# Residual rows kept transposed through the tail: scatter added to feature rows, norm factors applied behind the projections, gated outputs handed over one step later

## What is computed

```python
xl_new = xl + gt1 * (mix_l @ w_out)
xl_new = xl_new + gt2 * expert_choice_ffn(...)          # scatter: zeros.at[idx].add(ye)
x = rmsnorm(xl_new, g_final)                            # end of the first block
# even layer
h = rms_norm(x, g_in); z = h @ w_in                     # z: cq, ckv, kpe, q_s, k_s, v_s, gate
q = rms_norm(cq, g_q_a) @ w_q_up; kv = rms_norm(ckv, g_kv_a) @ w_kv_up
x = x + (concat(o_mla, o_swa) * silu(gate)) @ w_out
# odd layer
h = rms_norm(x, g_in); z = h @ w_in                     # z: q, k, v, forget logits, gate
x = x + (o * silu(gate)) @ w_out
out = rms_norm(x, g_final_2)
```

## Time and profile before

| what | value |
|---|---|
| time, three runs | 1425.26, 1425.86, 1425.97 us |
| profiled execution, its own time | 1426.7 us |
| span of its trace | 1424.9 us |
| PE, DVE, ACT, POOL busy | 991.3, 341.5, 245.9, 94.7 us |
| transfers | 483.21 MB, mean 339 GB/s |

### The profile page before, as it was taken

The page is one execution under the profiler, slowest core; times in us unless marked ns, Lnnn a source line. Parts: engine busy times, 40 slices in busy tenths (PEclk is TensorE's granted clock), DMA queues, the critical chain, the costliest instruction groups (busy, mean ns, idle before and its releaser), DMA issues.

```text
span 1424.9 us, 14616 instructions
## 1 busy us (share of the span) xinstructions
PE 991.3 (70%) x6385; PEld 490.5 (34%) x6385; DVE 341.5 (24%) x810; ACT 245.9 (17%) x501; POOL 94.7 (7%) x87
## 2 busy tenths in 40 slices
PE   5998876666565656665665576555655688889977
PEld 3855822212121111111111111111111587779875
DVE  4766500000001000000000000000000647645574
ACT  3534100000000000000000000000000546434442
POOL 1300000000020000000000000000000363100020
PEclk9999988878887787878878778888887799989999
DMA  9995689999999999999999999999998341144411
...
DMA packets 34992, 483.21 MB, mean 339 GB/s; under 512 B 3886, under 2 KB 3888, under 8 KB 5744
## 3 DMA queue, kind: packets, MB, share of 16 engines
...
q0 software_dynamic: 400, 1.31, 0.3%
...
HBM read 481.21 MB, written 1.05 MB: 338 GB/s over the span
## 4 chain that ended last, share of the span: by engine, by line
DMA 56%; PE 31%; DVE 7%; ACT 4%; issue 1%; POOL 0%; SPq 0%; POOLq 0%; DVEq 0%; ACTq 0%
DMA ring<-in_t_w 55%; PE PS L470 8%; PE PS L482 6%; PE PS L972 5%; PE PS L1019 2%; ACT S L595 2%; PE PS L459 1%; PE PS L741 1%; PE PS L659 1%; PE PS L763 1%; ACT RR L434 1%; DVE S L576 1%; PE PS L958 1%; PE PS L878 1%; PE PS L562 1%
## 5 line engine op out<-in xcount | busy, mean ns | idle before, releaser
L972 PE MATMUL PS<-ring,S 128*32 128x512 f32 x2048 | 322.4, 763 | 226.2 <-DMA ring<-in_t_w 223.7
L1019 PE MATMUL PS<-ring,S 128*32 128x512 f32 x1024 | 172.3, 807 | 109.9 <-DMA ring<-in_t_w 101.7
L972 PEld LDWEIGHTS PS<-ring,S 128*32 128x32 f32 x2048 | 63.1, 126 | 469.9 <-DMA ring<-in_t_w 346.7
L1019 PEld LDWEIGHTS PS<-ring,S 128*32 128x32 f32 x1024 | 33.5, 130 | 232.5 <-DMA ring<-in_t_w 155.7
L470 PE MATMUL PS<-RR,SR 128*128 128x512 f32 (+4 forms) x376 | 106.7, 389 | 8.2 <-DVE RR L1503 3.5
L490 ACT ACTIVATE S<-PS 128x512 f32<-128x512 f32 (+3 forms) x58 | 32.5, 565 | 371.9 <-PE PS L459 330.8
L482 PE MATMUL PS<-SR,RR 128*128 128x256 f32 x608 | 94.3, 283 | 2.2 <-DVE RR L1503 2.0
L434 ACT ACTIVATE RR<-ring 128x1024 fp32r<-128x1024 f32 (+3 forms) x95 | 89.4, 1004 | 6.2 <-DMA ring<-in_t_o_g 3.3
L1856 ACT ACTIVATE S<-PS 128x512 f32<-128x512 f32 x16 | 9.6, 597 | 453.9 <-PE PS L972 453.9
L482 PEld LDWEIGHTS PS<-SR,RR 128*128 128x128 f32 x608 | 85.1, 190 | 3.2 <-DVE RR L1503 2.4
L440 DVE TENSOR_TENSOR RR<-ring,RR 128x1024 fp32r<-128x1024 f32 (+2 forms) x72 | 81.6, 1185 | 8.1 <-ACT RR L434 8.0
...
## 6 DMA issues: line engine op xcount, KB each, us to landing
ring<-in_t_w SPq DMA_DIRECT2D x192, 2048.0 KB, 31.5
...
```

The source lines that it names most:

```text
L972: m = pe.e.matmul(PS[32 * j:32 * j + 32, b, :], XE[:, 2 * k + kk, 32 * e_:32 * e_ + 32], place[name, e_, k][:, kk, 512 * j:512 * j + 512], ...
L1019: m = pe.e.matmul(PS[q:q + 32, b, :], HT[e_ % 2][:, 128 * s + 32 * j:128 * s + 32 * j + 32], place["w2", e_, j][:, s, 512 * dh:512 * dh + ...
```

## The change

- **Experts.** The scatter is turned: `YE` is now the stationary operand and `GT` the moving one, so that its result has features on partitions (8 matmuls of 256 columns for 4 of 512). Its eight blocks are not added up in PSUM: DVE adds each at once to the transposed residual `XT` with the gate as a factor per partition (`add_rows`, 8 instructions per expert), behind `GT` of the next expert. `G2`, its two matmuls and its load go, and `copy_out` stands for the product. The gate comes from four small matmuls (`mod_cols("g")`) in the first attention. The broadcast load of `g_final` during the experts goes too.
- **To the even layer.** No transposes. `HE` is made from `XT` times `g_final*g_in` per partition, block by block as the last scatter lands, before the norm is known. `za` follows block by block. The norm comes later: ACT squares, 16 float32 matmuls (`ss`), DVE and POOL make the factors; DVE writes them on diagonals, four matmuls with ones spread them over the partitions (`spread_rows`), ACT copies them to `RB`. They are applied where results leave PSUM: `za`, `qst`, `kst`, `vs` and the gates. DVE writes the normed residual into `XT` (`x2`, 8 instructions, L1595 in the new kernel).
- **Gates.** DVE multiplies the gate block by `RB` (`gpre`), ACT writes the tanh back into PSUM, and DVE finishes it at the next turn; the bank is held over one more turn.
- **Loops.** `gated` moves one step later, its parts apart: the product after the first turn, the high part after ACT's copy-out, the low part at the step's end; the last group stands behind the loop.
- **To the odd layer.** `out2` has features on partitions and runs by halves of its input (heads of the sliding window first). DVE adds each block to `XT` (`x3_add`), ACT and DVE make `HO` from it block by block, and `q0` starts without a norm. 16 matmuls (`ms4`) behind the first half of `q0` and two of `spread_rows` give the factor, which is applied on the way out of PSUM, now on DVE alone for `q0` to `k1`. 16 transposes (`x3t`) behind `vf` bring the residual back to token rows.
- **Ring.** The tail's pairs of slots change from (0,1), (2,3), (4,5) to (5,0), (1,3), (4,2).

Walking the bank counter through both programs gives the bank of the first `za`: before bank 1, now bank 3, whose last holder is the scattered block 7 of the last expert, the last that is added. `ct` 0 and 2 stand in the banks of `qst` 0 and 1.

The core of the diff:

```diff
+    PAIRS = ((5, 0), (1, 3), (4, 2))
...
+            key = ("gates", a, half, n2)
+            dve.wait_ge(("tanh", a, half, n2))
+            v = PS[:, banks.of[key], :].rearrange("p (n t) -> p n t", n=2)
+            d = SGT[:, 4 * half + 2 * n2:4 * half + 2 * n2 + 2, :]
+            dve.e.scalar_tensor_tensor(out=d, in0=v, scalar=1.0, in1=d, op0=ALU.add, op1=ALU.mult).then_inc(
+                *dve.mark(("gate", a, half, n2), out_of(key)))
...
-                    dve.wait_ge(("tanh", a, half, n2))
+                    dve.wait_ge(("gates", a, half, n2), ("rb", a))
...
+                    dve.e.tensor_tensor(d, v, bc(RB[:, 0, :], [P, 2, 256], 1), ALU.mult).then_inc(
+                        *dve.mark(("gpre", a, half, n2)))
...
+            mod_cols("g")
...
+            for j in range(8 if e_ == E - 1 else 4):
+                banks.take(("sc", e_, j), ((4 + j) % 8,))
+            pe.wait_ge(("gt", e_), out_of(("w2", e_)), *[banks.was[scattered(e_, k)[0]] for k in range(8)])
...
+                    key, o = scattered(e_, 4 * dh + c)
+                    m = pe.e.matmul(PS[:, banks.of[key], o:o + 256], YE[e_ % 2][64 * dh:64 * dh + 64, 128 * c:128 * c + 128],
+                                    GT[e_ % 2][64 * dh:64 * dh + 64, :], start=True, stop=True)
...
         pe.stage("even")
-        pe.wait_ge("xf 0", "xf 1")
-        for m_ in range(4):
-            transposes(pe, ("HE", m_), ALL6, [XF[:, i, 128 * (2 * m_ + kk):128 * (2 * m_ + kk) + 128]
-                                              for kk in range(2) for i in range(2)])
-        pe.wait_ge(*[out_of(("HE", m_)) for m_ in range(4)])
-        for i in range(2):
-            project(pe, ("za", i), ("e", "a"), HE, i, 416, final=i == 1)
+        for i in range(2):
+            project(pe, ("za", i), ("e", "a"), HE, i, 416, ks=KORD, final=i == 1, first=[("he", k) for k in range(8)])
+        b = banks.take("ss", ALL6)
+        pe.wait_ge(banks.was["ss"], "gg", *[("sqs", c) for c in range(4)])
+        for i in range(2):
+            for k in KORD:
+                c, dh = k % 4, k // 4
+                m = pe.e.matmul(PS[:, b, 2 * i:2 * i + 2], sqs[:, c, 256 * dh + 128 * i:256 * dh + 128 * i + 128],
+                                gg[:, k, :], start=k == KORD[0], stop=k == KORD[-1])
+        m.then_inc(*pe.mark("ss"))
...
+            pe.wait_ge(banks.was[name, "rows"], (name, "dg"))
+            for r in range(n):
+                m = pe.e.matmul(PS[:, b, 128 * r:128 * r + 128], ones, dg[:, r, :], start=True, stop=True)
...
+                spread_rows("e", 4)
...
-        for i in (1, 0):
-            for h in range(2):
-                project(pe, ("out2", h, i), ("out2", h), OT, i, 512, ks=(4, 5, 6, 7, 0, 1, 2, 3), final=i == 0,
-                        first=[("e", "done", 2 if i else 3)] * 4 + [("e", "done", 1 if i else 0)] * 4)
+        for half in (1, 0):
+            pe.wait_ge(*[("e", "done", m_) for m_ in ((0, 1) if half else (2, 3))])
+            for n2 in range(4):
+                straight(pe, ("out2", n2, half), ("out2", n2 // 2), OT, n2 % 2, final=half == 0 and n2 % 2 == 1,
+                         ks=range(4 * half, 4 * half + 4))
...
+        straight(pe, ("q0", 0), ("o", "q0"), HO, 0, first="ho")
+        b = banks.take("ms4", ALL6)
+        pe.wait_ge(banks.was["ms4"], *[("sq3", n2) for n2 in range(4)])
+        for i in range(2):
+            for k in range(8):
+                m = pe.e.matmul(PS[:, b, i:i + 1], sqs[:, k // 2, 256 * (k % 2) + 128 * i:256 * (k % 2) + 128 * i + 128],
+                                gg[:, 0, 0:1], start=k == 0, stop=k == 7)
+        m.then_inc(*pe.mark("ms4"))
+        straight(pe, ("q0", 1), ("o", "q0"), HO, 1, final=True)
+        spread_rows("o", 2)
...
+                transposes(pe, ("x3t", i, h), ALL6, [XT[:, 4 * h + k, 128 * i:128 * i + 128] for k in range(4)])
...
+            t = dve.e.scalar_tensor_tensor(out=XT[:, k, :], in0=PS[:, banks.of[key], o:o + 256],
+                                           scalar=ab[:, 7, k:k + 1], in1=XT[:, k, :], op0=ALU.mult, op1=ALU.add)
...
+        for c in range(4):
+            dve.wait_ge(("scat", E - 1, c), ("xa", E - 2, 7))
+            for k in (c, 4 + c):
+                add_rows(E - 1, k)
+            lo_piece(dve, ("e", "a"), (0, 4, 2, 6)[c])
+            for k in (c, 4 + c):
+                dve.wait_ge(("he hi", k), "gg", ("xa", E - 1, k))
+                dve.e.scalar_tensor_tensor(out=HE[1][:, k, :], in0=XT[:, k, :], scalar=gfe[:, k:k + 1],
+                                           in1=HE[0][:, k, :].bitcast(F32), op0=ALU.mult,
+                                           op1=ALU.subtract).then_inc(*dve.mark(("he", k)))
+        lo_piece(dve, ("e", "qs"), 0)
+        lo_piece(dve, ("e", "qs"), 2)
+        dve.wait_ge("ss")
...
+        lo_piece(dve, ("e", "qs"), 4)
+        lo_piece(dve, ("e", "qs"), 6)
...
+            dve.e.tensor_tensor(dst[:, 2 * n2:2 * n2 + 2, :], PS[:, banks.of[name, n2], :].rearrange("p (n t) -> p n t", n=2),
+                                bc(RB[:, 0, :], [P, 2, 256], 1), ALU.mult).then_inc(*dve.mark(out_of((name, n2))))
...
+        for k in range(8):
+            t = dve.e.scalar_tensor_tensor(out=XT[:, k, :], in0=XT[:, k, :], scalar=c_gf[:, k:k + 1], in1=RB[:, 1, :],
+                                           op0=ALU.mult, op1=ALU.mult)
+        t.then_inc(*dve.mark("x2"))
...
+            ended = A2[n - 2] if n >= 2 and A2[n - 2]["last"] else None
+            if ended:
+                gated(dve, None, "e", ended, OT, ("product",))
...
-            if n and A2[n - 1]["last"]:
-                gated(dve, None, "e", A2[n - 1], OT)
+            if ended:
+                gated(dve, None, "e", ended, OT, ("low",))
         rest(side)
+        gated(dve, None, "e", A2[-1], OT, ("product", "low"))
...
+            dve.e.tensor_tensor(v, v, PS[:, banks.of[key], :].rearrange("p (n t) -> p n t", n=2), ALU.add).then_inc(
+                *dve.mark(("x3a" if half else "x3", n2), out_of(key)))
...
+        for n2 in range(4):
+            x3_add(n2, 0)
+            for k in (2 * n2, 2 * n2 + 1):
+                dve.wait_ge(("ho hi", k), ("x3", n2))
+                dve.e.scalar_tensor_tensor(out=HO[1][:, k, :], in0=XT[:, k, :], scalar=c_go[:, k:k + 1],
+                                           in1=HO[0][:, k, :].bitcast(F32), op0=ALU.mult,
+                                           op1=ALU.subtract).then_inc(*dve.mark(("ho", k)))
...
+        for c in range(4):
+            for k in (c, 4 + c):
+                act.wait_ge(("xa", E - 1, k), "gg")
+                act.e.activation(HE[0][:, k, :], XT[:, k, :], ACT.Copy, scale=gfe[:, k:k + 1]).then_inc(*act.mark(("he hi", k)))
+            if c < 2:
+                hi_piece(act, ("e", "a"), (2, 6)[c])
+        for c in range(4):
+            act.e.activation(sqs[:, c, :].rearrange("p (r t) -> p r t", r=2), XT[:, c:c + 5:4, :], ACT.Square).then_inc(
+                *act.mark(("sqs", c)))
...
-        pool.e.dma_start(gfb, A["g_final"].partition_broadcast(P)).then_inc(*landed("g_final"))
...
-        for i in range(2):
-            pool.e.tensor_scalar(X[:, i, :], XN3[:, i, :], rs_[:, i:i + 1], None, ALU.mult).then_inc(*pool.mark(f"x {i}"))
+        pool.wait_ge("rr")
+        pool.e.tensor_tensor(rr, rr, KC[:, K_HALF:K_HALF + 4], ALU.pow).then_inc(*pool.mark("ra"))
+        lo_all(pool, ("e", "kvs"))
```

338 lines of the change are left out of this document (163 added, 175 removed).

## The result

The changed kernel takes 1434.27 us (median, 1433.79 to 1435.45), the kernel before 1425.56 in the same comparison: ratio 1.0068, 95% interval 1.0056 to 1.008. The forecast was 1415.0, between 1405 and 1424. The profiled execution has a span of 1432.0 us, 7.1 more than before.

What follows compares the result with a forecast made beforehand. Only the 321 us tail counts: PE bounds the odd middle, a chain through DVE and ACT the loops. Terms 0.7 - 6.3 + 5.1 + 11.6 - 5.4 + 5.0 = +10.7 gave 1415 us, range 1405 to 1424.

Steps and rivals of the forecast that it cites:

- Head: Before the tail: four small matmuls cost 0.8 us at most, the dropped g_final broadcast saves about 1.5; gain 0.7.
- Front: From the last expert's copy to the even loop's start: 81.2 us instead of 74.9, loss 6.3.
- Rival B: In the front, x2 runs ahead of POOL's pieces; 7.6 us of wait go, net 7: 1408 us; chance 0.2.
- Even loop: Even layer's attention loop: handing finished parts over one step later gains 5.1 us, bounds -3 and +8.
- D: Both loops: DVE becomes the bound, gates cost it 5.5 us, handover gains nothing: 1431 us; chance 0.08.
- step 3: Third numbered step of the even loop: 11.95 us become a chain of 7.2 to 8.3; gain 4.7.
- step 1: Even loop: 2.8 us between the end of dividing and the next step become one instruction of 0.7; gain 2.1.
- To the odd layer: From out2 to q0: the 9.3 us window goes, 0.6 of out2 and 1.7 of slow q0; gain 11.6.
- Middle of the odd layer: PE-bound stretch before the odd loop: ms4 3.2 us, spreading 0.4, x3t 1.75 are added; loss 5.4.
- Odd loop: Odd layer's attention loop: same steps as the even loop with as much idle PE; gain 5.0 us.
- C: Both loops: scores, exponents, copy-out and values bound them, unshortened by the handover; they gain 1 us each: 1423; chance 0.17.

Runs made afterwards that it cites:

- e4_combined_small: Changed kernel with x2 behind the even loop, kp rotation early, gates finished at once, sums spread, norm first, POOL's pieces small, forget gate's copy earlier: 1406.01 us.
- gate_bank: Changed kernel, but the gates of the even loop's first step (half 1, second pair) take the next PSUM bank instead of bank 5: 1428.76 us.
- before_handover: Kernel before with only the handover: product, high and low part of a finished part stand one step later in both loops: 1414.71 us.
- small pieces: POOL's low parts cut into instructions of 256 columns, where they had 512 to 1024; on the kernel before with the handover: 1409.51 us.

## Why the prediction was wrong, step by step

Behind the experts 20 us lie between forecast (10 gained) and measurement (10.0 lost): 7.4 in the even loop, 4.4 in the front, 4.1 in the odd loop with the last projection, 4.0 between the loops.

**Head.** The 0.7 can't be told from nothing: the experts' end scatters by 4.7 us. The broadcast of g_final was not tried alone.

**Front.** The mechanism was right, some terms were too small. `za` began 10.85 us after the last expert's copy (10.0 said), x2 took 11.61 (11), PE idled 13.1 (13). Two terms were mis-sized: `ss` took 4.17, not 3.2, and qst's first half 8.18, not 5.7, because the clock fell in `ss`. `za` took 10.71, not 11.64, so that `qst` began only 0.9 late. Behind it x2 began 1.7 later than said (27.9 after qst, not 26.2), and x2 with the low parts of `ct` took 2.0 more (13.2, not 11.2): `qup` began 41.1 after qst (1126.56 to 1167.65), not 37.4. I had priced the small matmuls by four router matmuls (eight records) and given them no effect on what follows. The terms of `qst` to `vs` add up to 21.0, not 21.2, and before needed 19.6 for them, so they were 1.4 behind before and not 1.9; the total does not hang on it. Rival B had its condition, x2 began 0.93 us before POOL, but not its effect: three instructions went through, four were held. The front was also the place with most to win: e4_combined_small does it in 67.6.

**Even loop.** This is the step that failed most: +5.1 gained was forecast, 2.3 were lost. By the prediction's own sign (a loop above 53 us means D) the 54.9 spoke for D, but its cause was another. The handover gained 5.6 us, where 5.1 were forecast with the gates (the terms given add up to 5.2, with step 3 at the top of its own range). The rest of the change cost 1.7, near the 2.8 that rival D gave four gates. What the working left out is that a gate's bank is now held until a finish that stands behind `largest` of the next step, and that PE's scores queue behind the gates that want this bank. I costed step 1's DVE work at 0.7 for 2.8 and never asked who takes bank 5 next. The late finish cost 6.2 us, more than the handover brought, 4.3 of it by this one bank.

**To the odd layer.** Right in kind: no gap, 240 products in a row. Out2 and q0 became 4.4 us shorter with `ms4` (3.46) and the spreading (0.45) in them, so the pause and its consequences gave 8.3 of 11.6. Of the missing 3.3 the clock has 2.2: `out2` began at 0.50, and the 48 products behind `ms4` took 7.32 where they took 5.86 in gate_bank, whose stretch is 2.2 shorter. The last 1.1 are products that took 0.122 to 0.123 at full clock there, not 0.119.

**Middle of the odd layer.** Right: `ms4` 3.46 (3.2), spreading 0.45 (0.4), `x3t` 1.75 (1.75). The stretch grew by 2.3; the other 0.55 are spread over some 430 matmuls that ran about 1% slower. The wait of 0.57 for the forget gate's copy was there before (0.56).

**Odd loop.** The handover gained 3.0 of 5.0; the rest of the change (1.0) and the late finish (1.1) took 2.1 back. Here too transposes wait 3.03 us for a gate's finish; why the loop lost only 1.1 by it stays open.

**Rivals.** D named 1431, next to the result, but not its cause: the handover gained 8.6 us in the two loops, and all but the late finish cost 2.7 there, where D gave DVE's extra instructions 5.5. C is out as well, since before_handover shortened both loops by more than 1 us. The range was too narrow because its ends were B's x2 beside POOL and C's loops; none stood for a bank held longer or for a slower clock.

What stays open: what decides whether PE's clock falls behind `ms4` (in gate_bank it did not, in six other kernels with the block it did), why small pieces made the even loop of before_handover 2.1 us longer and its odd loop with out3 3.1 shorter, and what the transposed even front is worth against the transposed odd transition.
